# Five joints between stages in two halves of the tokens: last outputs, norm chain and the next stage's first four groups by 256 columns

## What is computed

```
for i in range(4):
    g = norm_g[i]
    hn = _rms(x, g[0])
    m = conv mixer (i = 0, 3), pool mixer (i = 1) or differential attention (i = 2) of hn
    x = x + _rms(m, g[1])
    f = (silu(_rms(x, g[2]) @ w_gate[i]) * (_rms(x, g[2]) @ w_up[i])) @ w_down[i]
    x = x + _rms(f, g[3])
```

## Time and profile before

| | |
|---|---|
| median of 3 runs | 2789.2 us |
| the profiled execution | 2790.27 us |
| its span | 2788.4 us |
| granted TensorE clock | 0.996 |
| PE busy | 2745.3 us (98%) |
| VectorE busy | 1326.0 us (48%) |
| GpSimd busy | 1233.4 us (44%) |
| ScalarE busy | 939.1 us (34%) |
| HBM read | 281.08 MB |

### The profile page before, as it was taken

The page is one execution under the profiler, slowest core; times in us unless marked ns, Lnnn a source line. Parts: engine busy times, 40 slices in busy tenths (PEclk is TensorE's granted clock), DMA queues, the critical chain, the costliest instruction groups (busy, mean ns, idle before and its releaser), DMA issues.

```text
span 2788.4 us, 37011 instructions
## 1 busy us (share of the span) xinstructions
PE 2745.3 (98%) x13784; PEld 2278.2 (82%) x13784; DVE 1326.0 (48%) x1825; ACT 939.1 (34%) x1318; POOL 1233.4 (44%) x913
## 2 busy tenths in 40 slices
PE   8999999999999999999999999999999999999997
PEld 6888877887888888888888888878888888888886
DVE  3344675668455441175441276565441174544413
ACT  4443447743133222252222334342222221422222
POOL 3444442134535545515555433235454454454554
PEclk9999999999999999999999999999999999999999
DMA  9556231122323333313333321223333333233333
GB/s 317 162 192 192 74 124 54 32 61 76 98 76 106 96 97 101 112 69 113 91 97 105 98 89 59 61 62 113 98 98 101 103 91 91 83 106 97 91 106 98
DMA packets 106252, 285.09 MB, mean 102 GB/s; under 512 B 38734, under 2 KB 38862, under 8 KB 104852
## 3 DMA queue, kind: packets, MB, share of 16 engines
q1 hardware_dynamic: 99360, 257.64, 30.7%
q10 hardware_dynamic: 6771, 25.74, 2.6%
HBM read 281.08 MB, written 8.85 MB: 104 GB/s over the span
## 4 chain that ended last, share of the span: by engine, by line
issue 41%; PE 34%; POOL 23%; DVE 1%; POOLq 0%; DMA 0%; ACT 0%; ACTq 0%; DVEq 0%
POOL w_lo L644 23%; PE ps L450 11%; PE ps L452 11%; PE ps L451 11%; DVE x L2551 0%; DMA hot_raw<-in_onehot 0%; DVE tmp L2545 0%; POOLq L642 0%; PE ps L503 0%; POOLq L166 0%; PE ps L751 0%; PE ps L766 0%; PE ps L729 0%; PE ps L531 0%; PE ps L514 0%
## 5 line engine op out<-in xcount | busy, mean ns | idle before, releaser
L644 POOL TENSOR_TENSOR w_lo<-w_raw,w_hi 128x512 fp32r<-128x512 f32 x904 | 1232.5, 1386 | 1544.2 <-ACT w_hi L443 1544.2
L450 PE MATMUL ps<-u_hi,w_hi 128*128 128x512 f32 x2256 | 885.2, 392 | 9.5 <-DVE u_lo L2294 6.4
L452 PE MATMUL ps<-u_hi,w_lo 128*128 128x512 f32 x2256 | 878.2, 389 | 0.0
L451 PE MATMUL ps<-u_lo,w_hi 128*128 128x512 f32 x2256 | 877.9, 389 | 0.0
L443 ACT ACTIVATE w_hi<-w_raw 128x1024 fp32r<-128x1024 f32 x452 | 475.3, 1055 | 779.5 <-PE ps L452 741.6
L450 PEld LDWEIGHTS ps<-u_hi,w_hi 128*128 128x128 f32 x2256 | 423.5, 188 | 104.6 <-DVE u_lo L2294 10.8
L452 PEld LDWEIGHTS ps<-u_hi,w_lo 128*128 128x128 f32 x2256 | 423.4, 188 | 88.8
L451 PEld LDWEIGHTS ps<-u_lo,w_hi 128*128 128x128 f32 x2256 | 423.6, 188 | 88.3 <-issue 1.9
L450 PE MATMUL ps<-h_hi,w_hi 128*128 128x512 f32 (+1 forms) x726 | 277.9, 383 | 0.0
L452 PE MATMUL ps<-h_hi,w_lo 128*128 128x512 f32 (+1 forms) x726 | 277.8, 383 | 0.0
L451 PE MATMUL ps<-h_lo,w_hi 128*128 128x512 f32 (+1 forms) x726 | 277.7, 383 | 0.0
(11 more groups left out here) (342 smaller groups left out, 3003.6 us busy)
## 6 DMA issues: line engine op xcount, KB each, us to landing
w_raw<-in_stream SPq DMA_DIRECT2D x452, 512.0 KB, 3.6
late_ring<-in_ada_late ACTq DMA_DIRECT2D x32, 512.0 KB, 5.3
ada_ring<-in_ada SPq DMA_DIRECT2D x8, 1024.0 KB, 17.6
dilated_bias_rows<-dilated_bias SPq DMA_DIRECT2D x18, 244.1 KB, 6.2
band_a<-dilated_bias_rows SPq DMA_DIRECT2D x96, 28.0 KB, 2.0
x<-in_x SPq DMA_DIRECT2D x8, 256.0 KB, 17.5
bias_rows<-bias_scratch ACTq DMA_DIRECT2D x4, 512.0 KB, 7.8
out_yT<-x SPq DMA_DIRECT2D x8, 256.0 KB, 2.0
```

Of the source, the lines that this page charges most:

```text
L450: nc.tensor.matmul(o, w[0], v[0], start=start, stop=False)
L451: nc.tensor.matmul(o, w[0], v[1], start=False, stop=False)
L452: return nc.tensor.matmul(o, w[1], v[0], start=False, stop=stop)
L644: ins = nc.gpsimd.tensor_tensor(w_lo[:, s, half], w_raw[:, s, half], w_hi[:, s, half].bitcast(F32), ALU.subtract)
```

## The change

Five joints are treated alike: conv 0 to FFN 0, FFN 1 to the attention, the attention to FFN 2, FFN 2 to conv 1, conv 1 to FFN 3. The other joints (into conv 0, into and out of pool) and the end of FFN 3 stay.

On PE `halved_tail` makes the last outputs (two after a conv mixer or the attention, one after an FFN) first for tokens 0 to 255 in their old banks, then for tokens 256 to 511 in banks 4 and 5. The first half's sums and spread stand inside the second pass, ahead of its products 3 and 7. `opening_halves` makes the next stage's first four groups for the first half: groups 0 and 1 on tiles 0 to 2, the second half's sums, groups 2 and 3 on tiles 0 to 2, all four on tiles 3 to 7, with the second half's spread behind tile 3; then all four for the second half. `pe_factor` and its filler go from these joints.

```diff
+            def half_sums(half, acc_again=False):
+                if half == 0 or acc_again:
+                    pe.wait_ge(acc_ready, n.up("acc"))
+                for r in range(2 * half, 2 * half + 2):
+                    pe.matmul(bank(7, P, at=r * P), acc[:, r * P:(r + 1) * P], ones[:, :], ...)
+                pe.wait_ge(y_last_sq, n.up("last"))
+                for r in range(2 * half, 2 * half + 2):
+                    mm = pe.matmul(bank(7, P, at=r * P), sq[:, 1, r * P:(r + 1) * P], ones[:, :], ...)
+                mm.then_inc(y_sums, 1)
...
+            def halved_tail(starts, nk, parts, banks, evacuated):
+                for half, w in enumerate(HALVES):
+                    if half:
+                        pe.wait_ge(out_evac, evacuated)
+                    for i, c0 in enumerate(starts):
+                        for k in range(nk):
...
+                            if half and nk * i + k == 3:
+                                half_sums(0)
+                            if half and nk * i + k == 7:
+                                half_spread(0, 6)
+                            mm = product(bank(JOINT_B_BANKS[i] if half else banks[i], 2 * P, at=0),
+                                         chunk_tiles(c % RING, t), (hi[:, w], lo[:, w]), k == 0, k == nk - 1)
+                            if half and (t == TPC - 1 or k == nk - 1):
+                                mm.then_inc(chunk_used, 1)
...
+            def opening_halves(c0, acc_again):
+                for k in range(3):
+                    pe.wait_ge(u_half, n["uh"] - KD + k + 1)
+                    unit(k, 0, 0)
+                    unit(k, 1, 0)
+                half_sums(1, acc_again)
+                for j in (2, 3):
+                    for k in range(3):
+                        unit(k, j, 0)
+                for k in range(3, KD):
+                    pe.wait_ge(u_half, n["uh"] - KD + k + 1)
+                    for j in range(4):
+                        unit(k, j, 0)
+                    if k == 3:
+                        half_spread(1, 7)
...
```

```diff
+                act.wait_ge(half_done, n.up("half", len(banks)))
+                half_square(0, banks[-1])
+                half_root(0)
+                if two:
+                    first(0)
+                    chunk(stage, rest[0])
+                    square_before_last(1)
+                    first(1)
+                else:
+                    chunk(stage, rest[0])
+                    first(0)
+                    first(1)
+                    chunk(stage, rest[1])
+                first(2)
+                if not two:
+                    first(3)
+                act.wait_ge(chunk_used, used)
+                half_square(1, JOINT_B_BANKS[len(banks) - 1])
+                begin(nxt_stage)
...
+                scaled_parts(*nxt, w=SECOND)
```

On DVE `finish_halves` takes the place of `finish`:

```diff
+                for t in range(KD):
+                    add_y(t, 0)
+                    if t + 1 < KD:
+                        scaled_y(t + 1, 0)
+                    if two and t == 0:
+                        copy_before_last(1)
+                    if t:
+                        first_half_tile(nxt[0], nxt[1], t - 1)
+                    if two and t == 2:
+                        add_before_last(1)
+                    if t == 4:
+                        copy_last(1)
+                factor(1)
+                first_half_tile(nxt[0], nxt[1], KD - 1)
...
+                scaled_y(0, 1)
+                for t in range(KD):
+                    add_y(t, 1)
+                    if t + 1 < KD:
+                        scaled_y(t + 1, 1)
+                    next_parts(nxt, t + 1, SECOND)
```

More of the change, by code:

```diff
@@ L1112, in out8 @@
                             mm.then_inc(chunk_used, 1)
-                for m in range(2, KD):
+                for m in range(2, KD - 2 if halved else KD):
                     if m >= 4:
@@ L1785, in _, with half_square @@
             layernorm_parts(1, "conv_in0", False, (0, 0))
-            def out_squares(stage):
-                for m in range(KD):
-                    chunk(stage, m)
-                    if m < KD - 1:
-                        out_square(m)
-                last_square(BASE[stage] + KD, (KD - 1) % 4)
+            def half_square(half, b):
+                act.wait_ge(sq_used, n["squ"] - 1)
+                nc.scalar.activation(sq[:, 1, HALVES[half]], bank(b, 2 * P), ACT.Square).then_inc(y_last_sq, 1)
@@ new lines, in half_root, with square_before_last @@
+            def half_root(half):
+                act.wait_ge(y_sums, n.up("last"))
+                c = 2 * half
+                nc.scalar.activation(col[:, 12 + c:14 + c], summed(7)[:, c:c + 2], ACT.Sqrt, bias=eps_rms[:, 0:1],
+                                     scale=1.0 / D).then_inc(dev_ready, 1)
+            def square_before_last(half):
+                act.wait_ge(y_half, n.up("yh"))
+                square_slot()
+                nc.scalar.activation(sq[:, 0, HALVES[half]], y[:, KD - 2, HALVES[half]],
+                                     ACT.Square).then_inc(sq_ready, 1)
@@ L1795, in last_square, with out_squares @@
+            def out_squares(stage, banks, nxt, nxt_stage):
+                for m in range(KD - 2):
+                    if m or stage not in begun:
+                        chunk(stage, m)
+                    out_square(m)
+                chunk(stage, KD - 2)
+                joint(nxt, nxt_stage, stage, (KD - 1,), BASE[stage] + KD, banks)
             def last_square(used, b):
@@ L1879, in conv @@
                 rounds(act, 2, in_body)
-                out_squares(f"conv_out{which}")
-                finish(nxt, stage)
+                out_squares(f"conv_out{which}", (2, 3), nxt, stage)
             conv(0, (0, 2), "up0")
@@ L1968, in _ @@
             c_norm(LAST)
-            for m in range(KD):
-                if m:
-                    chunk("c_out", m)
-                if m < KD - 1:
-                    out_square(m)
-            last_square(BASE["c_out"] + KD, C_OUT_BANKS[KD - 1])
-            finish((2, 2), "up2")
+            begun.add("c_out")
+            out_squares("c_out", C_OUT_BANKS[6:], (2, 2), "up2")
             ffn(2, (3, 0), "conv_in1")
```

234 lines of the change are left out of this document (174 added, 60 removed).

## The result

The changed kernel takes **2805.7 us** (median of 6 runs, 2804.38 to 2806.73) against 2789.1 for the kernel before: ratio 1.0058, 95% interval 1.0047 to 1.0068. It is slower by 16.6 us. The forecast was 2797.8, so the direction was right and the size half of what came; the result lies 0.7 us above the range.

The account below looks back on a forecast made before the run. PE, busy 98%, was taken as the bound; waits from DVE and POOL collisions outweighed the saved gaps, 3 x 2.2 + 2 x 1.0 = +8.6 us, giving 2797.8 us. The range was 2782.5 to 2805.

Parts of the forecast that it names:

- What bounds the kernel: Whole kernel: PE is busy 98% of the span, so only its issued work and its waits or filler can move time.
- PE's own ledger: PE at five joints: without waits, two-output joints go 40.54 to 38.09, FFN joints 44.62 to 42.41; ceiling 11.8 us gained.
- What collides: Opening: POOL's weight splits alternate with DVE's additions, square additions and u_lo, one locked DVE instruction per 1.4 us.
- 1.41 less 0.42 leaves 1.0 held: DVE beside POOL, last group: hold of 1.0 us per instruction, where a POOL instruction alone takes 1.25.
- The joint's waits: PE's u_lo waits: two-output joints 1.9 and 1.6 to 3.0 us; FFN joints 0.2 and 1.5, then 1.1 for the fourth chunk.
- The wait for the second factor: Two-output joints: second factor up to 0.5 us late, as its reciprocal stands behind seven u_lo.
- These finish about when PE wants their sum: no cost: Opening's end: whole-width square additions on DVE, 0.69 each, cost nothing, with under 1 us of slack.
- Rival (3), the clock: Joints without filler: bare PE waits up to 3 us drop the clock, 2.9 more per joint, 2812 us; chance 0.09.
- the row at 634.61 speaks against it for short waits: PE at 634.61: it waited 1.85 us and the clock of 620 to 640 stayed 1.00, taken against a clock fall.
- The sum: Five joints: 3 x 2.2 for two-output plus 2 x 1.0 for FFN joints gives +8.6 us, median 2797.8.

Follow-up runs that it names:

- best version: Changed kernel with product and squares in PSUM, opening's last three tiles by column, second half's root and reciprocal earlier, its u_lo one tile behind: 2784.35 us, ratio 0.9982.
- the bare-wait runs: Kernel before without pe_spread's filler: 2802.6 us; changed kernel with three filler matmuls ahead of tile 2 only, tile 1's wait bare: 2801.67 us.
- the joints with filler: Changed kernel with four and three useless matmuls ahead of PE's waits for tiles 1 and 2 in the two-output joints: 2800.71 us.
- product in PSUM: Changed kernel with the first half's scaled output written to a free half bank of PSUM, before its addition to x: 2795.76 us, ratio 1.0021.
- quarters: Changed kernel with GpSimd's low parts of twelve weight chunks in four instructions of 256 columns instead of two of 512: 2800.1 us.
- the four runs with quarters and the product in SBUF: Changed kernel, 256-column weight low parts: alone 2800.1 us; plus filler 2798.86; plus last three tiles by column 2797.96; plus reordered squares, sums and spread 2804.87.

## Why the prediction was right or wrong

- **What bounds the kernel** (PE's waits and gaps only) was right: five joints carry 15.3 of 15.9 us.
- **PE's own ledger** was right within what can be read. The best version's two-output joints take 39.1 us, 1.0 over the 38.09 of "PE never waits", and two waits for u_lo with 0.51 and 0.73 between starts are still in them; slots of 0.120 stand wherever PE runs dense at full clock.
- **What collides** was right in mechanism and near in size: one locked DVE instruction per GpSimd instruction, 1.10 for u_lo (forecast 1.4 for a cycle) and 1.5 for an addition. The working "1.41 less 0.42 leaves 1.0 held" was not sound, as the 1.41 has a scaling in it: the row at 2773.48 shows 0.56 held, and only the longest of that source view, 1.46, shows 1.0. The Trainium skill ("SBUF — State Buffer", SBUF: two separate sides) names as exposed a VectorE operation with two SBUF inputs. That is the set that the runs show: addition, square addition and u_lo held, scaling and `x<-x,ps` not. Its block for the whole of the other's instruction, at most 1.25 here, agrees with an excess of 1.1 for an addition and 0.6 for u_lo, since VectorE's instruction came when POOL's was already under way: an addition of 0.42 behind the POOL instruction that began at 814.56 would end at 816.23, and it ended at 816.27.
- **The joint's waits** were sized a little high: 1.78 and 1.28 for 1.9 and 1.6 to 3.0; the FFN joints' 1.23 and 0.81 for 1.5 and 1.1. The wait for the second factor did not show, as it lay under the others until they were gone.
- **"These finish about when PE wants their sum: no cost"** was wrong, by 0.9 us in each of five joints. Two waits with restarts, of 0.50 and 0.63 between starts where 0.12 to 0.24 is normal, stand at the opening's end. The additions are not held in the changed kernel. DVE's chain is late with bare durations, 1.42 us for two: the column copy starts at 844.04, and PE was free for the sum at 843.86. And the fifth chunk is free late, since the halves free chunks every 0.72 us at the very end: POOL starts on it at 843.82, and PE gets to it at about 845.9. The step left the chunk out, and put the chain's cover at "under 1 us" without pricing it gone.

```profile
842.59 1.42 DVE L2446 TENSOR_TENSOR acc<-acc,tmp 128x512 f32<-128x512 f32 x2
844.04 0.15 DVE L2450 COPY col<-acc 128x1 f32<-128x1 f32 x1
...
843.82 6.31 POOL L652 TENSOR_TENSOR w_lo<-w_raw,w_hi 128x512 fp32r<-128x512 f32 x5 [22.73 <-ACT w_hi L451]
```

- **Rival (3), the clock**, got 0.09 and came true in part: 4.6 us, in the three joints with two bare waits. The step that failed is "the row at 634.61 speaks against it for short waits": that row is of *one* wait, and the prediction itself forecast two close together. The Trainium skill ("TensorE: Matmul & The Clock Gate", What's actually happening) has the clock released by activity and throttled otherwise; the bare-wait runs agree with that in kind, by 13 us in the kernel before.
- **The sum**: 8.6 forecast. Clock 4.6 and the end 4.4 come on top, and the waits sized too high take 2.3 off (the joints with filler, where the clock held, cost 10.7 over the kernel before): 15.3, as the joints show. The other 1.3 of the 16.6 us lie outside them and stay unexplained. The range left out rival (3) altogether; had two waits of 1.6 to 1.9 been treated as its case, it would have held the result.

Not tried: the clock's fall with other spacings of two waits, and squares in PSUM in the kernel before, so part of the best version's gain may be had without the halves. Nor was the scaling's later place, with its product left in SBUF.

## What to carry to other kernels

When a gap on the bounding engine is closed by overlap, list what else ran in that gap: here GpSimd's weight parts, harmless as long as VectorE's chain had the stretch almost to itself, came to lie on it and cost 19 us. Where the two must overlap, let VectorE's second input come from PSUM: that took the hold off the additions for half a bank of PSUM, where shorter GpSimd instructions only shortened it and made GpSimd itself later. Filler that looks idle may be what keeps TensorE's clock; if a change removes it, price every bare wait that it leaves, and several close together as more than one.

## What was not expected of the hardware

- Of additions beside GpSimd, those with one input in PSUM take 0.42 us, those with both in SBUF 1.50. Twice 512 columns go from 2.40 to 1.41.
- GpSimd pays as well: two chunks take 5.82 us beside held operations, 5.56 beside fewer, and 7.32 in eight instructions of 256 columns.
- The length of a bare wait on TensorE does not settle the clock by itself. In the profiled executions those of 1.85 us, 1.87 (product in PSUM) and 1.63 (quarters) left it alone, and one of 1.77 brought it down in one joint of three. Those of 2.15 in the FFN joints of the four runs with quarters and the product in SBUF brought it down four times out of eight.
- With the two waits of 1.78 and 1.28, PE's products ran at the low clock for 3.3 us in two joints and 5.8 in a third, with the same instructions.
